# New step sequences for both blocks and the gdn stage of a two-layer decoder kernel

## What is computed

```
def gla_attention(q, k, v, log_a):
    ...
    def step(state, inp):
        qc, kc, vc, gc = inp
        b = jnp.cumsum(gc, axis=-2)
        o_inter = jnp.einsum('bhcd,bhde->bhce', qc * jnp.exp(b), state)
        diff = b[:, :, :, None, :] - b[:, :, None, :, :]
        decay = jnp.exp(jnp.where(mask[None, None, :, :, None], diff, -jnp.inf))
        att = jnp.einsum('bhid,bhjd,bhijd->bhij', qc, kc, decay)
        o_intra = jnp.einsum('bhij,bhje->bhie', att, vc)
```

## Time and profile before

| what | us |
|---|---|
| timed runs: median (lowest to highest) | 1418.52 (1418.11 to 1419.04) |
| profiled execution, its own time | 1420.49 |
| its span, first to last instruction | 1418.7 |
| PE busy | 1396.4 |
| DVE busy | 1024.2 |
| ACT busy | 992.2 |

### The profile page before, as it was taken

One profiled execution on the slowest core, in us unless ns is written; L12 is line 12 of the kernel. 1 busy time (PEld: TensorE's weight loads), 2 busy tenths in 40 slices (PEclk: granted clock), 3 DMA queues, 4 the chain that ended last, 5 costly groups with the idle time before them and its releaser, 6 DMA issues.

```text
span 1418.7 us, 20586 instructions
## 1 busy us (share of the span) xinstructions
PE 1396.4 (98%) x7875; PEld 1146.4 (81%) x7875; DVE 1024.2 (72%) x1413; ACT 992.2 (70%) x1762; POOL 69.5 (5%) x163
## 2 busy tenths in 40 slices
...
GB/s 227 167 144 93 142 203 119 119 137 190 186 200 192 181 188 193 147 206 199 189 197 178 193 192 194 191 169 185 136 164 104 125 123 90 165 206 199 188 205 92
DMA packets 168290, 238.26 MB, mean 168 GB/s; under 512 B 21554, under 2 KB 114640, under 8 KB 168192
## 3 DMA queue, kind: packets, MB, share of 16 engines
...
q10 hardware_dynamic: 64, 0.02, 0.0%
...
## 4 chain that ended last, share of the span: by engine, by line
PE 94%; DVE 2%; ACT 2%; DMA 1%; issue 0%; SPq 0%; DVEq 0%; ACTq 0%
PE A L245 18%; PE A L246 17%; PE A L247 17%; PE G L247 5%; PE G L245 5%; PE G L246 5%; PE M L246 5%; PE M L245 5%; PE M L247 5%; PE A L1331 1%; PE G L1252 1%; PE G L1299 1%; DVE tmp L414 1%; PE M L1309 1%; DVE x_lo L419 1%; ACT x_hi L399 1%
## 5 line engine op out<-in xcount | busy, mean ns | idle before, releaser
L227 DVE TENSOR_TENSOR w_lo<-raw,w_hi 128x1024 fp32r<-128x1024 f32 (+2 forms) x296 | 507.0, 1727 | 122.4 <-ACT w_hi L209 121.8
L209 ACT ACTIVATE w_hi<-raw 128x1024 fp32r<-128x1024 f32 (+2 forms) x296 | 427.1, 1462 | 126.4 <-DMA raw<-in_ffn_w_gate_up 97.7
L245 PE MATMUL A<-w_hi,x_hi 128*128 128x512 f32 (+1 forms) x640 | 259.3, 405 | 3.5 <-DVE x_lo L419 1.2
L247 PE MATMUL A<-w_hi,x_lo 128*128 128x512 f32 (+1 forms) x640 | 247.7, 387 | 0.0
L246 PE MATMUL A<-w_lo,x_hi 128*128 128x512 f32 (+1 forms) x640 | 246.9, 386 | 0.0
L690 ACT ACTIVATE ffn_ffn_hT<-ffn_ffn_hb 32x128 f32<-32x128 f32 x512 | 157.1, 307 | 11.7
L245 PEld LDWEIGHTS A<-w_hi,x_hi 128*128 128x128 f32 x640 | 120.7, 189 | 33.4 <-DVE x_lo L419 6.7
L247 PEld LDWEIGHTS A<-w_hi,x_lo 128*128 128x128 f32 x640 | 120.4, 188 | 25.3
L245 PE MATMUL A<-w_hi,ffn_ffn_hT_hi 128*128 128x512 f32 x352 | 139.0, 395 | 0.0
L246 PE MATMUL A<-w_lo,ffn_ffn_hT_hi 128*128 128x512 f32 x352 | 138.3, 393 | 0.0
L246 PEld LDWEIGHTS A<-w_lo,x_hi 128*128 128x128 f32 x640 | 120.9, 189 | 21.2 <-issue 0.7
...
## 6 DMA issues: line engine op xcount, KB each, us to landing
...
```

Source lines behind the costliest of these rows:

```text
L209: ins = act.activation(net.w_hi[:, v % RING, part], net.raw[:, v % RING, part], ACT.Copy)
L227: ins = dve.tensor_tensor(net.w_lo[:, v % RING, part], net.raw[:, v % RING, part], net.w_hi[:, v % RING, part].bitcast(F32), ALU.subtract)
L245: pe.matmul(out, xh, hi[:, k, c, :], start=start and k == 0, stop=False)
L247: mm = pe.matmul(out, xl, hi[:, k, c, :], start=False, stop=stop and k == nk - 1)
```

## The change

The three lists are replaced. Every step of the old lists is in the new ones, once; PE's sequence of units and quarters is the same. What differs is between which quarters the other steps stand, and in which order they stand to each other. Cut to the lines that the argument speaks of (the rest of the lists changes in the same manner):

```diff
 FIRST_ORDER = """
     mempre
-    unit:mem:0:0 keep:1 keep:0
-    unit:mem:0:1 keep:2 rms:mem hi:2:0 lo:2:0 hi:2:1
-    unit:mem:0:2
-    unit:mem:0:3
-    unit:mem:1:0 lo:2:1
-    unit:mem:1:1 keep:3 hi:3:0 xpre hi:3:1 lo:3:0 evac:mem
-    unit:mem:1:2 hi:4:0 hi:4:1
-    unit:mem:1:3 lo:3:1 rms:x
+    unit:mem:0:0 rms:mem
+    unit:mem:0:1 keep:0 keep:2 lo:2:0 keep:1 lo:2:1
+    unit:mem:0:2 hi:2:0
+    unit:mem:0:3 hi:2:1 keep:3 hi:3:0
+    unit:mem:1:0 xpre hi:3:1
+    unit:mem:1:1 lo:3:0 evac:mem hi:4:0 lo:3:1
+    unit:mem:1:2
+    unit:mem:1:3
     unit:gr:0:0
     unit:gr:0:1
-    unit:gr:0:2 evac:gr hi:5:0 lo:4:0
-    unit:gr:0:3 lo:4:1
+    unit:gr:0:2 hi:4:1
+    unit:gr:0:3 rms:x
+    unit:gr:1:0
+    unit:gr:1:1 evac:gr
+    unit:gr:1:2
+    unit:gr:1:3 hi:5:0 lo:4:0 hi:5:1
+    unit:b:0:0 lo:4:1
...
+    out:1:0:3 lo:21:0 next:lo:6 hi:21:0 lo:21:1 hi:21:1 next:lo:7 add:1
...
 SECOND_ORDER = """
...
-    unit:ka:0:0 hi:11:1 evac:qa norm1:qm hi:12:0 glav:0 gate1:m hi:12:1 norm2:qm norm1:qa glav:1 levels:1:0 turn:mk
...
+    unit:ka:0:0 glav:0 glav:1 hi:12:0 hi:12:1 levels:1:0
+    unit:ka:0:1
+    unit:ka:0:2 hi:13:0
+    unit:ka:0:3 turn:mk norm2:qm norm2:qa gate2:b levels:1:1
...
-    out:1:0:1 fpre:g:0 hi:21:1 fpre:l:0 fpre:h:1 fpre:t:0 fpre:g:1 lo:21:0 fpre:l:1 fpre:t:1 add:1
-    out:1:0:2 lo:21:1
...
+    out:1:0:1 fpre:t:0 fpre:h:1 fpre:t:1 fpre:g:1 add:1
+    out:1:0:2 fpre:l:1 lo:21:0 lo:21:1
     out:1:0:3
 """.split()
...
 GDN_ORDER = """
...
-    unit:q1:1:0 hi:9:1 hi:10:0 kd:3:0 kd:3:1 l2:k1:0 silu:k1:1:1
-    unit:q1:1:1
-    unit:q1:1:2 l2:k1:1 evac:q1:0
-    unit:q1:1:3 lo:9:0 lo:9:1 lo:10:0 lo:10:1 hi:10:1 ba:2 norm:k1:0 blocks:0 norm:k1:1 conv:q0:0 conv:q0:1
-    unit:v0:0:0
...
+    unit:q1:1:0 kd:3:1 lo:9:0
+    unit:q1:1:1 hi:10:1 silu:k1:1:1 lo:9:1 norm:k1:0 ba:2
+    unit:q1:1:2
+    unit:q1:1:3 lo:10:0 lo:10:1 l2:k1:1 evac:q1:0 norm:k1:1 blocks:0 conv:q0:0 evac:q1:1
+    unit:v0:0:0 conv:q0:1
...
-    unit:v1:0:1 hi:14:0 solved:0
...
-    unit:v1:1:1 evac:v1:0 spread:0 kk:4:1 lo:13:1
...
+    unit:v1:1:2 lo:13:1 kd:4:0 kd:4:1 solved:0 hi:14:1 evac:v1:1 silu:q1:1:0 silu:q1:0:1 l2:q1:0 spread:0 lo:14:0
...
-    unit:z2:1:2 z1:z0:2 hi:24:0 hi:24:1 core:4:x2 core:5:x2 vt:v3:0 z2:z0:2 vt:v3:1
...
+    unit:z2:1:1 core:4:x2 z1:z0:2 core:5:x2 z2:z0:2 vt:v3:0 hi:24:1
...
-    out:5:1 lo:31:0 z1:z3:2 z2:z3:2 lo:31:1 lo:32:0 hi:32:0 hi:32:1
-    out:5:2 ot:6
-    out:5:3 ot:7 lo:32:1
+    out:5:1
+    out:5:2 z1:z3:2 lo:31:1
+    out:5:3 z2:z3:2 hi:32:0 lo:32:0 hi:32:1 ot:6 ot:7 lo:32:1
 """.split()
```

More of the change, by code:

```diff
@@ new lines @@
+    unit:m:0:0
+    unit:m:0:1 norm2:mk
+    unit:m:0:2 evac:b kexp turn:qkb
+    unit:m:0:3 hi:8:0 lo:7:1
+    unit:m:1:0 hi:8:1 hi:9:0 hi:9:1 evac:m
+    unit:m:1:1
+    unit:m:1:2
+    unit:m:1:3 gate1:b spread lo:8:0 lo:8:1 lo:9:0 levels:0:0
+    unit:qa:0:0
+    unit:qa:0:1
+    unit:qa:0:2 lo:9:1 hi:10:0 levels:0:1 lo:10:0
+    unit:qa:0:3 hi:10:1 hi:11:0 hi:11:1 evac:qa
+    unit:qa:1:0
+    unit:qa:1:1 norm1:qm hi:12:0 turn:mk hi:12:1 levels:0:2 hi:13:0
+    unit:qa:1:2 lo:10:1
+    unit:qa:1:3 lo:11:0 norm1:qa glav:0 glav:1 levels:1:0
@@ L845 @@
[L845 to L848, removed]
-    unit:qa:0:0
[L850 to L869, removed]
+    unit:m:0:1 evac:b kexp lo:7:0
+    unit:m:0:2 turn:qkb
+    unit:m:0:3 hi:8:0 gate1:b hi:8:1 lo:7:1
+    unit:m:1:0 spread lo:8:0 hi:9:0
@@ L885 @@
+    out:0:1:3 jgate:2
     out:1:1:0
[L886 to L892, removed]
-    out:0:0:1
[L894 to L897, removed]
@@ L898 @@
-    out:1:0:3 next:lo:7 add:1
-""".split()
-SECOND_ORDER = """
[L903 to L943, removed]
-    unit:ka:0:0 hi:11:1 evac:qa norm1:qm hi:12:0 glav:0 gate1:m hi:12:1 norm2:qm norm1:qa glav:1 levels:1:0 turn:mk
[L945 to L980, removed]
-    out:1:0:1 fpre:g:0 hi:21:1 fpre:l:0 fpre:h:1 fpre:t:0 fpre:g:1 lo:21:0 fpre:l:1 fpre:t:1 add:1
-    out:1:0:2 lo:21:1
@@ L1921 @@
 GDN_ORDER = """
[L1922 to L1928, removed]
-    unit:k1:0:2
-    unit:k1:0:3 lo:5:0 l2:k0:0 lo:5:1 hi:6:0 evac:k1:0 silu:k0:1:1 ba:0
-    unit:k1:1:0
-    unit:k1:1:1
-    unit:k1:1:2
-    unit:k1:1:3 lo:6:0 hi:6:1 evac:k1:1 norm:k0:0
-    unit:q0:0:0 lo:6:1 l2:k0:1 conv:k1:0
```

320 lines of the change are left out of this document (208 added, 112 removed).

## The result

The new kernel is slower: 1421.38 us in the median of 20 runs (1420.12 to 1423.54) against 1419.26 for the kernel before (1417.68 to 1421.31), a ratio of 1.0014 (95% interval 1.0008 to 1.0020), so 2.0 us (1.1 to 2.8). The forecast was 1418.2 us, 0.3 us faster than the 1418.5 then known. The time lies inside the range, but on the other side of the kernel before. The profiled executions took 1420.74 us after and 1420.49 before; the one of before holds a stretch at half clock and the one after doesn't.

The account below looks back on a forecast made before the run. TensorE, busy 98% of the span, was taken as the bound, so order could move only roughly 22 us of idle time. Terms -0.6 + 0 - 1.0 + 0 + 1.3 = -0.3 took 1418.5 to 1418.2 us; range 1414.9 to 1422.6.

Parts of the forecast that it names:

- Block 0: In block 0, two waits go (-0.8, -0.5) and one comes ahead of xpre (+0.7): net -0.6 us.
- Both waits: In block 0, TensorE's waits for evac:mem (0.8 us, unit gr) and lo:4 (0.5 us, unit b) go.
- the new wait: In block 0, TensorE stands ahead of xpre for ACT's copy keep:3: 0.7 us, bounds 0 to 1.3.
- Block 1 and the joints: In block 1 and at its end, no wait to lose: 0, with 1.2 us of loss as the bound.
- gdn, first half: In the first half of the gdn stage, a wait and small gaps go: -1.0 us.
- "-0.7" and "-0.3": In gdn's first half, the wait ahead of conv:q0:1 goes (-0.7 us) and q0's norm products quicken (-0.3 us).
- The slower rival's chain at norm:k1:1: Mid-gdn, DVE and ACT queues delay norm:k1:1's square; TensorE takes over 3.4 us: 1422.6 us, chance 0.20.
- gdn, the first inverse: In gdn, solved:0 and spread:0 come a quarter later, the data still in time: 0, bounds 0 to +1.0 us.
- The end: At gdn's end, the first product behind ot:7 waits for ot:6's x_lo: +1.3 us, bounds 0.9 to 2.3.
- a second late w_lo: At gdn's end, lo:32's 1.2 us might fall in between, taking the wait to its upper bound, 2.3 us.
- The clock: Near 225 us, a shorter row of small products and transposes would lose the half-clock stretch of 1.7 us.
- The rivals: Whole kernel: slower by queues 1422.6 us (0.20), faster as removable waits go 1415.3 (0.18), slow clock stretches 1420.8 (0.10).

Follow-up runs that it names:

- f1: New kernel with its last three gdn lines, core:4:p4, core:6:x2, solved:0 and spread:0 as in the kernel before; 0.9994 of the kernel before.
- e2: Kernel before with only the new lists of the two blocks; 0.9995 of the kernel before.
- e8: Kernel before with only conv:q0:1 moved behind unit:v0:0:0; 1.0003 of the kernel before.
- e11: New kernel with solved:0 and spread:0 back where the kernel before has them; 1.0010 of the kernel before.
- e6: New kernel with core:4:p4 and core:6:x2 one quarter earlier, as the kernel before has them; 1.0006 of the kernel before.
- e7: Kernel before with only core:6:x2 one quarter later, behind core:7:t2; 1.0013 of the kernel before.
- e3: New kernel with z2:z3:2 and ot:6 moved back in front of out:5:3; 1.0015 of the kernel before.
- e9: Kernel before with TensorE's instructions shifted by 144 through idle semaphore waits ahead of feed-forward quarters; 1.0022 of the kernel before.
- e10: New kernel with TensorE's instructions shifted by 200 through idle semaphore waits ahead of feed-forward quarters; 1.0002 of the kernel before.
- f0: New kernel unchanged, timed again in the last group; 1.0012 of the kernel before.
- f2: Kernel before with the new list of block 0 and 232 idle waits on TensorE ahead of feed-forward quarters; 0.9994 of the kernel before.
- e4: New kernel with 112 tiny matmuls ahead of TensorE's first product; 1.0048 of the kernel before.

## Why the prediction was wrong

The forecast was -0.3 us and the change was +2.0. Two terms of the sum were wrong and one place was not in it; the time of the kernel before was also put too low.

- **Block 0**: right. Forecast -0.6, measured -0.6 in the new kernel's lag. Both waits went. ACT came to evac:mem only 0.5 us sooner (29.57 for 30.07), not 1.4; that was enough because TensorE itself came there 0.8 us later, after the new wait. Ahead of xpre TensorE stood for 0.7 us in f1 and 0.9 in e2, as "issue", 0.2 in the new kernel's profile, where TensorE was late itself by 0.5 us of slow clock at the start. Forecast 0.7.
- **Block 1 and the joints**: right, 0.
- **gdn, first half**: wrong step. Forecast -1.0, measured -0.2. "-0.7" and "-0.3" treated a wait that goes as time gained. I named nothing that is late next. The chain from the taps to the square of q0 on ACT and DVE did not start sooner, and it took most of the gain back (e8: 0.1 left of 0.8; the new kernel: 0.2, with the new wait of 0.4 at norm:q0:0). The slower rival's chain at norm:k1:1 did not come about: TensorE passed there without a wait.
- **gdn, the first inverse**: wrong step. Forecast 0, measured +0.4. I asked only whether the spread's data would be in time. It was. What the later spread held up were the weight loads behind it in SP's queue, and with their burst a block of TensorE's instructions came late (e11; that the one delayed the other is inferred).
- **The second half of gdn**: not in the sum, that is put at nothing because TensorE was busy for 168.85 of 169 us there. Measured +0.8. No wait had to be there for a new one to arise: moving core:6:x2 by one quarter used up a block of TensorE's instructions before the next had come (0.7 to 0.9 in e6, 1.6 in e7 the other way). The trace of before had the hint, a row of L2475 of 0.76 us for 32 small matmuls where rows like it take 0.4, and I read it as nothing.
- **The end**: right, forecast +1.3, measured 1.2 to 1.4. The bound of a second late w_lo held too: it stood behind the first (e3).
- **The time of the kernel before**: the 1418.5 us came of three timed runs. The 20 beside the new kernel have a median of 1419.26: 12 took 1417.7 to 1419.5 us, the other 8 1420.3 to 1421.3. So 0.7 us of the distance to 1418.2 is the base and not the change.
- **The clock**: the transposes in a row do not decide the stretch at 225 us. It stands in 6 of the 18 profiles, with the old list of block 1 (the kernel before, e9) and with the new one (e2, e10, e11, f1), and is absent in others of both lists; f0 and f2 have one at 79 us in its place, e4 has two, at 20 and 85. The rule of the Trainium skill cited in the prediction is neither confirmed nor refuted by that. Taking the stretch out of the profiled execution but not out of the runs was only partly right. The median run was said not to hold it; but in the last group 15 timed runs of the kernel before with a granted clock of 0.999 or more took 1417.7 to 1419.1 us, and 18 with 0.998 took 1419.9 to 1421.1. So it seems that about half of them hold such a stretch somewhere.
- **The rivals**: the time fell inside the range, 1414.9 to 1422.6, but by luck: the range reached up so far for the sake of a chain at norm:k1:1 that did not come about. Of the 2.0 us, 1.2 stand behind entries of TensorE's instruction stream, which none of my cases had.
